# Retention in chunks of 128 instead of 256 tokens, with seven f32 accumulators, and the sample projections moved up

## The chip, the cores and the metric

The kernel runs as one program on all 8 cores of one Trainium2 chip. Each core works on its own share of the data and no core waits for another. The time is the device time in microseconds (us) of the slowest core. The engines are named as in the profile: PE (TensorE, matmuls; PEld are its weight loads), DVE (VectorE), ACT (ScalarE), POOL (GpSimd) and SP (SyncE, which here only issues DMAs).

## The reference, cut to what matters

One layer of a hybrid decoder serves 8 prompts of 2048 tokens and 128 short sequences ("samples") of 8 tokens. Every layer has three branches (retention, a short convolution, cross-attention into memory), which are merged by gates and projected. The change is in the retention branch alone:

```python
def step(S, blk):                       # chunks of RET_CHUNK = 128 tokens
    qc, kc, vc = blk
    s = jnp.einsum('bihd,bjhd->bhij', qc, kc) * inner[None]
    o = (jnp.einsum('bhij,bjhe->bihe', s, vc)
         + jnp.einsum('bihd,bhde->bihe', qc, S) * q_dec[None, :, :, None])
    S = (S * chunk_dec[None, :, None, None]
         + jnp.einsum('bjhd,bjhe->bhde', kc * k_dec[None, :, :, None], vc))
    return S, o
...
o = o * lax.rsqrt(jnp.mean(o * o, axis=-1, keepdims=True) + EPS) * ret_norm_g
```

q and k are rotated (rotary embedding) before this; there are 4 heads with 256 key and 256 value channels. S is the recurrent state of a head, 256 x 256 numbers. The result does not depend on the length of a chunk, since the formula is exact for any length, so a kernel is free to choose it. The samples go through the same formula with one chunk of 8 tokens and a state from memory, which is also written back.

## The kernel before

Each core takes one prompt (2048 tokens, in 4 groups g of 512) and 16 samples (128 tokens in all). The stages run one after the other: normalisation and transposes, the convolution branch with its projection, the memory branch with its projection (`projM`), the retention branch, its projection (`projR`), and the output projection. A small planner (`Plan`) records every operation in program order. Each engine executes its own operations strictly in that order; the planner adds a semaphore wait where an operation reads or overwrites what another engine has written or still reads. A tile is tracked as a whole or in blocks, so a wait can be wider than the data needs.

PSUM, which takes the results of PE, has 8 banks. Six of them (`psf`) are f32 accumulators of 128 x 512, two (`psh`) take transposes. `falloc` and `ffree` hand out the accumulators first in, first out, while the program is built. So it is fixed beforehand which earlier user each accumulator had, and PE waits until the last reader of that user is done.

The retention stage is a loop over i = 0 to 15, that is 4 heads h times 4 groups g. I call one turn of it a period, and number its steps:

1. `prot(i, 256)`: the K projection (16 matmuls of 512 columns into two accumulators). DVE then multiplies by cosine and sine (L1107, four operations of 128 x 512) and POOL subtracts and adds (L1110, L1113). This is the K rotation.
2. `fins`: for the period before, DVE multiplies the normalised output by the gate (L1335, four operations) and so frees its two accumulators.
3. `qdec`: POOL multiplies q by its decay (L1245, two operations of 128 x 512). The table comes by DMA (`tables`, L1088 and L1089).
4. Four `vg_tile` (8 matmuls of 512 columns each): values and gates. ACT copies the values (L1255) and takes the SiLU of the gates (L1256) into `gsg1`, which `fins` reads; so ACT's first SiLU of a period waits for `fins`. After the third tile come the 8 transposes of K (`k_trans`), which ACT scales into `kdt1` (L1266, four operations).
5. `r_scores`: k times q for two chunks of 256 tokens, as three blocks of 128 x 128 each, and the mask on DVE (L1282).
6. `tail(i - 1)`: 8 transposes of the output of the period before, which ACT scales into `ob` (L1238).
7. `kv_state`, twice: the new contribution to the state on PE; DVE updates the f32 state `S32` (L1296, or the copy L1299 for the first chunk of a head). `kv_cast` is ACT's bf16 copy of `S32` (L1304). It reads what the next update overwrites, so update, cast and next update go one after the other. The second cast of a period is recorded only after step 10.
8. `prot(i + 1, 0)`: the Q projection of the next period and its rotation, as in step 1.
9. The samples' step: ACT casts their state (`s_cast`, L1164, two operations of 128 x 1024), PE multiplies (`s_out`, L1175) and computes the update (`s_upd`, two calls with two accumulators each), DVE adds it (L1191), SP writes it out and loads the next (`s_load`).
10. `o_chunk`, twice: 14 matmuls of 256 columns into two accumulators; ACT takes squares (L1200), DVE and POOL make the scale (L1202, L1204).

In the first period of a head (g = 0) the samples' q, k and v projections (`samp_a`) stand between the second and third `vg_tile`, and `samp_b` (transposes of their k, the masked copy `kdm` on DVE (L1148), scores and mask (L1157)) and `samp_d` (the samples' output, L1225) stand after step 7. `samp_a(0)` runs ahead of the loop. At the end of a head SP writes `S32` to memory (`nrp`, L1307), and the first state of the next head (L1299) must wait for that write. `mm` (L416) and `tr` (L419) are the helpers under which every matmul and transpose stands in the profile.

## Time and profile before

| | us |
|---|---|
| median of 3 runs | 1253.17 (1251.75 to 1255.77) |
| the profiled execution, its own time | 1262.68 |
| its span on the slowest core (core 1) | 1261.1 |
| spans of all cores | 1238.0 to 1261.1 |
| retention loop on core 1, first K projection to the end of step 10 of i = 15 | 718.36 to 1074.81 of the span |

The profile is one execution. Its times run from the first instruction of core 1. In a timeline a row gives the start, the length, the engine, the line, the operation with its output and inputs, how many instructions are merged, and in brackets how long the engine stood idle before it and which operation ended that. Engine busy times on core 1 are PE 1190.1, DVE 585.2, ACT 461.1 and POOL 332.6 us.

### The profile page before, as it was taken

To read this page: it belongs to the slowest core of one execution; us is meant where nothing else is said; L and a number is where in the kernel's file an instruction comes from. 1 tells how busy PE (TensorE), PEld (TensorE's weight loads), DVE (VectorE), ACT (ScalarE), POOL (GpSimd) and SP (SyncE) were. 2 spreads that over 40 slices of the span, in tenths; PEclk is the share of its full clock that TensorE was granted. 3 is DMA by queue.
4 is the path that set the end of the run, shared out by engine and by line. 5 is a ranking of instruction groups with operands and counts; after the bars stand their busy time and mean duration, and the time that the engine had idled before them with its cause. 6 is when DMAs were issued, how large, how long until landed. Compare 5 with 4: busy or idle time off the path is not lost.

```text
span 1261.1 us, 22033 instructions; the slowest of 8 cores (1238.0 to 1261.1 us)
## 1 busy us (share of the span) xinstructions
PE 1190.1 (94%) x7140; PEld 605.1 (48%) x7140; DVE 585.2 (46%) x1058; ACT 461.1 (37%) x1010; POOL 332.6 (26%) x424
## 2 busy tenths in 40 slices
PE   3889999999999999999999999989989799999997
PEld 1444444445554554554444544545545445444443
DVE  3764444442222355556212356556565565322266
ACT  3442233322222444444211254545445346322233
POOL 2332222221000111011333434435334344333300
PEclk9999999999999999999999999989999999999989
DMA  9734111112555686974421033724734633811074
GB/s 219 189 85 67 35 34 35 34 34 39 100 101 101 121 135 114 150 120 82 114 52 34 15 104 128 197 96 137 201 118 145 159 126 106 246 35 34 2 253 164
DMA packets 38000, 134.34 MB, mean 107 GB/s; under 512 B 4736, under 2 KB 8960, under 8 KB 33024
## 3 DMA queue, kind: packets, MB, share of 16 engines
q0 software_dynamic: 10080, 56.63, 27.0%
q1 hardware_dynamic: 27808, 76.30, 18.4%
q8 instruction: 60, 0.98, 0.3%
q14 instruction: 52, 0.43, 0.1%
HBM read 160.56 MB, written 28.98 MB: 150 GB/s over the span
## 4 chain that ended last, share of the span: by engine, by line
PE 75%; DVE 7%; DMA 6%; ACT 5%; issue 4%; SPq 1%; POOL 1%; DVEq 0%; ACTq 0%; POOLq 0%
PE psf L416 73%; DVE tf L1107 3%; DMA pms<-c_maskX 2%; DMA nrp<-arF 2%; DMA arF<-c_cos 1%; PE psh L419 1%; DMA mgd<-xp 1%; ACT th L944 1%; ACT ob L1238 1%; ACT arH L1304 1%; ACT mgd L476 1%; DVE th L953 1%; DVE mgd L485 0%; DVE ssb L940 0%; ACT arH L1164 0%
## 5 line engine op out<-in xcount | busy, mean ns | idle before, releaser
L416 PE MATMUL psf<-hT,w 128*128 128x512 bf16 (+1 forms) x3456 | 694.1, 355 | 3.1 <-ACT hT L499 1.5
L416 PEld LDWEIGHTS psf<-hT,w 128*128 128x128 bf16 x3456 | 315.7, 99 | 336.4 <-issue 44.9
L416 PE MATMUL psf<-ob,w 128*128 128x512 bf16 (+1 forms) x960 | 200.1, 352 | 0.0
L556 ACT ACTIVATE tf<-psf,hbg 128x512 f32<-128x512 f32 (+1 forms) x95 | 60.2, 633 | 210.7 <-PE psf L416 206.7
L416 PEld LDWEIGHTS psf<-ob,w 128*128 128x128 bf16 x960 | 87.8, 99 | 93.5 <-issue 12.0
L416 PE MATMUL psf<-w,hT 128*128 128x512 bf16 (+1 forms) x608 | 130.3, 368 | 1.1 <-ACT th L944 1.1
L567 DVE SCALAR_TENSOR_TENSOR tf<-tf,psf 128x512 f32<-128x512 f32 (+1 forms) x79 | 48.0, 607 | 176.2 <-PE psf L416 168.0
L571 POOL TENSOR_TENSOR mgd<-tf,mgd 128x512 bf16<-128x512 f32 (+1 forms) x79 | 78.8, 1005 | 160.1 <-DVE tf L567 160.1
L1107 DVE TENSOR_TENSOR tf<-psf,arF 128x512 f32<-128x512 f32 (+1 forms) x160 | 95.7, 610 | 29.0 <-POOL arH L1110 7.4
L416 PEld LDWEIGHTS psf<-w,hT 128*128 128x128 bf16 x608 | 59.3, 99 | 59.9 <-issue 6.1
L1110 POOL TENSOR_TENSOR th<-tf 128x512 bf16<-128x512 f32 x32 | 40.7, 1270 | 157.2 <-DVE tf L1107 122.2
L397 POOL DMA_DIRECT2D w<-wb x38 | 21.9, 577 | 171.2 <-PE psf L416 170.9
L416 PE MATMUL psf<-w,mgd 128*128 128x512 bf16 x272 | 62.2, 394 | 0.0
L416 PE MATMUL psf<-arH 128*128 128x256 bf16 (+1 forms) x232 | 39.8, 284 | 17.6 <-DVE tf L1107 15.0
L1282 DVE TENSOR_TENSOR arH<-psf,pms 128x256 bf16<-128x256 f32 x64 | 22.9, 358 | 64.3 <-PE psf L416 59.3
L1255 ACT CAST arH<-psf 128x256 bf16<-128x256 f32 x64 | 23.6, 369 | 67.5 <-PE psf L416 66.8
L416 PEld LDWEIGHTS psf<-w,mgd 128*128 128x128 bf16 x272 | 27.4, 101 | 34.4 <-issue 10.9
L1113 POOL TENSOR_TENSOR th<-tf 128x512 bf16<-128x512 f32 x32 | 40.7, 1271 | 4.9 <-DVE arH L1335 0.4
L944 ACT ACTIVATE th<-psf,ssb 128x256 bf16<-128x256 f32 x64 | 30.4, 474 | 27.0 <-DVE ssb L940 16.4
L1245 POOL TENSOR_TENSOR th<-th,pms 128x512 bf16<-128x512 bf16 x32 | 37.2, 1161 | 5.9 <-DMA pms<-c_qdecX 3.6
L419 PE MATMUL psh<-idb,mgd 128*128 128x128 bf16 x136 | 12.4, 245 | 26.5 <-DVE mgd L485 26.5
L1256 ACT ACTIVATE xbuf<-psf 128x256 f32<-128x256 f32 x64 | 24.6, 385 | 31.7 <-DVE arH L1335 26.9
(180 smaller groups left out, 1183.5 us busy)
## 6 DMA issues: line engine op xcount, KB each, us to landing
w<-wb POOLq DMA_DIRECT2D x38, 1024.0 KB, 10.8
mgd<-xp SPq DMA_DIRECT2D x16, 512.0 KB, 11.9
arH<-cmk POOLq DMA_DIRECT2D x12, 512.0 KB, 17.1
arH<-cmv POOLq DMA_DIRECT2D x10, 512.0 KB, 11.8
gaux<-sret SPq DMA_DIRECT2D x8, 512.0 KB, 4.4
xbuf<-sret SPq DMA_DIRECT2D x8, 512.0 KB, 5.1
stgt<-sret SPq DMA_DIRECT2D x8, 512.0 KB, 4.6
hbt<-sret SPq DMA_DIRECT2D x8, 512.0 KB, 5.7
```

Source lines behind the costliest of these rows:

```text
L416: P.op('pe', lambda e: e.matmul(out, lhsT=lhsT, rhs=rhs, start=start, stop=stop), reads=reads, writes=[wbuf])
L419: P.op('pe', lambda e: e.transpose(out=out, in_=in_, identity=ident), reads=reads + [B_id], writes=[wbuf])
L556: P.op('act', lambda e, fg=fg, ti=ti, n=n, bcol=bcol: e.activation(out=tf[ti][:, 0:n], in_=psf[fg][:, 0:n], func=AF.Tanh, bias=hbg[:, bcol ...
L567: P.op('dve', lambda e, fy=fy, ti=ti, t2=t2, n=n: e.scalar_tensor_tensor(out=tf[t2][:, 0:n], in0=tf[ti][:, 0:n], scalar=1.0, in1=psf[fy][: ...
L571: P.op('pool', lambda e, t2=t2, n=n, fc=fc, g=g: e.tensor_tensor(out=mgd[:, fc, sl(g)], in0=tf[t2][:, 0:n], in1=mgd[:, fc, sl(g)], op=ALU. ...
L944: P.op('act', lambda e, c=c, f=fs[hf]: e.activation(out=th_[pi][:, c * 256:(c + 1) * 256], in_=psf[f][:, (c % 2) * 256:(c % 2) * 256 + 256 ...
L1107: P.op('dve', lambda e, t=t, p_=p_, c_=c_: e.tensor_tensor(out=tf[t][:, 0:n], in0=p_, in1=c_, op=ALU.mult), reads=[B_psf[fps[f]], Bcs], wr ...
L1110: P.op('pool', lambda e: e.tensor_tensor(out=lo, in0=tf[b1][:, 0:n], in1=tf[b2][:, 0:n], op=ALU.subtract), reads=[B_tf[b1], B_tf[b2]], wri ...
L1113: P.op('pool', lambda e: e.tensor_tensor(out=hi_, in0=tf[a1][:, 0:n], in1=tf[a2][:, 0:n], op=ALU.add), reads=[B_tf[a1], B_tf[a2]], writes= ...
L1245: P.op('pool', lambda e, dch=dch: e.tensor_tensor(out=th_[qdi][:, dch * 512:(dch + 1) * 512].rearrange("p (c i) -> p c i", c=2), in0=th_[q ...
L1255: P.op('act', lambda e: e.copy(out=vtm1[:, c, :], in_=psf[f][:, 0:256]), reads=[B_psf[f]], writes=B_vtm1)
L1256: P.op('act', lambda e: e.activation(out=gsg1[:, c, :], in_=psf[f][:, 256:512], func=AF.Silu), reads=[B_psf[f]], writes=B_gsg1)
```

## The change

A chunk is now 128 tokens (`RC2 = 128`), so a period has four chunks with four state updates in place of two. The scores are four blocks of 128 x 128 in one accumulator with one masking operation, and `qdec` and the scaling of `kdt1` are one operation each. The state has four bf16 copies. One of the two transpose banks becomes a seventh f32 accumulator. The samples' projections stand right behind K (q and k in one accumulator, rotated in four operations of 256 columns), `samp_b` stands behind the second `vg_tile`, the two `s_cast` stand behind the first and the second `vg_tile`, and `tail` stands behind the Q projection. The write of `nrp` is issued right behind the last state update of a head.

```diff
-RC2 = 256
+RC2 = 128
...
+        psf.append(psh[1][:].bitcast(F32)); B_psf.append(B_psh[1])
+        free_h[:] = [0]
+        free_f.append(6)
...
         def samp_a(h):
-            proj_rot(h, 0, slice(LP, NT), 128, csS, BL_csS, qS[:, 0:128], qS[:, 128:256], BL_qS)
-            proj_rot(h, 256, slice(LP, NT), 128, csS, BL_csS, kS[:, 0:128], kS[:, 128:256], BL_kS)
+            fq = falloc()
+            for z in range(4):
+                off = (z // 2) * 256 + (z % 2) * 128
+                for k in range(8):
+                    mm(psf[fq][:, z * 128:z * 128 + 128], WA[:, k, off:off + 128], hT[:, k, LP:NT], k == 0, k == 7, [B_hT, BWA], B_psf[fq])
...
+            for (t, d, z) in ((0, 0, 0), (1, 1, 1), (2, 0, 1), (3, 1, 0)):
+                P.op('dve', lambda e, t=t, d=d, z=z: e.tensor_tensor(out=tv[t], in0=pv_[:, :, d, :], in1=cb[z], op=ALU.mult),
+                     reads=[B_psf[fq], BL_csS], writes=[B_tf[ts[t]]])
...
             fv = falloc()
-            for (o_, w0) in ((0, 0), (256, 256)):
-                for k in range(8):
-                    mm(psf[fv][:, o_:o_ + 256], hT[:, k, LP:NT], WB[:, k, w0:w0 + 256], k == 0, k == 7, [B_hT, BWB], B_psf[fv])
+            for k in range(8):
+                mm(psf[fv][:], hT[:, k, LP:NT], WB[:, k, :], k == 0, k == 7, [B_hT, BWB], B_psf[fv])
...
 # r_scores
+            fs = falloc()
             for c in range(4):
+                for dch in range(2):
+                    o_ = dch * 512 + c * 128
+                    mm(psf[fs][:, c * 128:(c + 1) * 128], th_[ki][:, o_:o_ + 128], th_[qi][:, o_:o_ + 128], dch == 0, dch == 1,
+                       [B_th[ki], B_th[qi]], B_psf[fs])
+            P.op('dve', lambda e: e.tensor_tensor(
+                out=stm1.rearrange("p (c t) -> p c t", c=4), in0=psf[fs][:, 0:512].rearrange("p (c t) -> p c t", c=4),
+                in1=maskX.unsqueeze(1).to_broadcast([128, 4, RC2]), op=ALU.mult),
+                reads=[B_psf[fs], B_mq], writes=B_stm1)
...
 # the loop
+            if g == 0 and h > 0:
+                samp_a(h)
             qdec(qi, qdi)
             vg_tile(WB, BWB, g, 0)
+            s_cast(h, g, 0)
             vg_tile(WB, BWB, g, 1)
-            if g == 0 and h > 0:
-                samp_a(h)
+            s_cast(h, g, 1)
+            if g == 0:
+                samp_q(h)
+                samp_b(h)
...
-            r_scores(ki, qi, sx)
-            if i > 0:
-                tail(i - 1)
+            r_scores(ki, qi)
...
-            kv_state(h, 2 * g)
-            kv_cast(h, 2 * g)
-            kv_state(h, 2 * g + 1)
-            if g == 0:
-                if h > 0:
-                    samp_d(h - 1)
-                samp_b(h)
+            for c in range(4):
+                kv_state(h, 4 * g + c)
+                if c < 3 or g == 3:
+                    kv_cast(h, 4 * g + c)
+            if g == 0 and h > 0:
+                samp_d(h - 1)
...
             if i < 15:
                 qn = prot(i + 1, 0)
...
-            s_cast(h, g)
+            if i > 0:
+                tail(i - 1)
             s_out(h, g)
...
-            fo = [o_chunk(2 * g, qdi, sx), o_chunk(2 * g + 1, qdi, sx)]
-            kv_cast(h, 2 * g + 1)
+            fo = [o_pair(h, g, qdi, 0), o_pair(h, g, qdi, 1)]
+            if g < 3:
+                kv_cast(h, 4 * g + 3)
```

`o_pair` makes two chunks of output in one accumulator: for each chunk one matmul of masked scores times values and two of decayed q times the state copy `Sbf[c]`.

## Rows read from the trace of the kernel before

**Rows 1.** Span and granted TensorE clock of the slowest core

```profile
core 1: 1261.1 us, clock 0.972
```

**Rows 2.** Windows: the loop, then periods 4, 8, 12 and 6

```profile
core 1: us, PE busy (x) PEld busy (x) DVE busy (x) ACT busy (x) POOL busy (x), PEclk, DMA share, GB/s
718.36:1074.81 356.45, 325.29 (x2165) 176.47 (x2163) 214.66 (x405) 173.79 (x426) 145.30 (x136) 0.96 0.48 137
801.25:830.42 29.17, 25.35 (x179) 14.58 (x177) 17.80 (x39) 13.15 (x34) 11.03 (x13) 0.89 0.51 140
892.37:921.19 28.82, 25.52 (x179) 14.75 (x177) 17.90 (x39) 13.00 (x34) 11.05 (x13) 0.91 0.53 147
981.94:1014.13 32.19, 24.62 (x180) 14.09 (x178) 17.74 (x39) 13.01 (x34) 10.97 (x13) 0.90 0.49 133
852.09:872.07 19.98, 18.79 (x128) 10.13 (x126) 12.70 (x24) 10.73 (x27) 8.39 (x8) 1.00 0.38 132
```

**Rows 3.** Timeline of PE, period 6 and the start of period 7

```profile
864.30 1.03 PE L416 MATMUL psf<-arH 128*128 128x256 bf16 x8
865.17 3.62 PE L416 MATMUL psf<-hT,w 128*128 128x512 bf16 x16
...
870.53 0.27 PE L416 MATMUL psf<-arH 128*128 128x256 bf16 x1 [1.06 <-DVE tf L1107]
...
872.07 3.62 PE L416 MATMUL psf<-hT,w 128*128 128x512 bf16 x16
```

**Rows 4.** Timeline of DVE, period 6 into 7

```profile
863.50 1.75 DVE L1282 TENSOR_TENSOR arH<-psf,pms 128x256 bf16<-128x256 f32 x4 [3.83 <-PE psf L416]
865.16 0.68 DVE L1296 SCALAR_TENSOR_TENSOR arF<-arF,psf 128x512 f32<-128x512 f32 x1
866.66 0.69 DVE L1296 SCALAR_TENSOR_TENSOR arF<-arF,psf 128x512 f32<-128x512 f32 x1 [0.82 <-ACT arH L1304]
867.31 0.69 DVE L1107 TENSOR_TENSOR tf<-psf,arF 128x512 f32<-128x512 f32 x1
868.17 2.21 DVE L1107 TENSOR_TENSOR tf<-psf,arF 128x512 f32<-128x512 f32 x3 [0.17 <-DVE tf L1107]
870.30 1.47 DVE L1191 SCALAR_TENSOR_TENSOR gaux<-gaux,psf 128x512 f32<-128x512 f32 x2
...
877.55 2.25 DVE L1335 SCALAR_TENSOR_TENSOR arH<-psf,ssb,xbuf 128x256 bf16<-128x256 f32 x4
```

**Rows 5.** Timeline of ACT, periods 6 and 7

```profile
867.40 1.04 ACT L1164 CAST arH<-xbuf 128x1024 bf16<-128x1024 f32 x1
...
879.89 0.38 ACT L1256 ACTIVATE xbuf<-psf 128x256 f32<-128x256 f32 x1 [2.02 <-DVE arH L1335]
880.17 0.37 ACT L1255 CAST arH<-psf 128x256 bf16<-128x256 f32 x1
...
883.68 0.47 ACT L1266 ACTIVATE arH<-psh,arF 128x256 bf16<-128x256 bf16 x1 [0.37 <-ACT arH L1266]
884.05 0.36 ACT L1255 CAST arH<-psf 128x256 bf16<-128x256 f32 x1
```

**Rows 6.** Waits of period 8 (first of a head): DVE, then PE

```profile
902.90 0.29 DVE L1107 TENSOR_TENSOR tf<-psf,arF 128x128 f32<-128x128 f32 x1 [1.13 <-POOL arH L1110]
912.59 0.69 DVE L1299 COPY arF<-psf 128x512 f32<-128x512 f32 x1 [1.98 <-DMA nrp<-arF]
...
916.26 0.27 PE L416 MATMUL psf<-arF 128*128 128x256 bf16 x1 [1.16 <-DVE arF L1157]
```

**Rows 7.** Timeline of SP's queue, end of period 3 into 4

```profile
806.10 0.33 SPq L1089 DMA_DIRECT2D pms<-c_qdecX  x1
...
815.49 0.42 SPq L1307 DMA_DIRECT2D nrp<-arF  x1
```

**Rows 8.** Windows of half clock after period 4, of the last wait of period 6

```profile
827.00:833.80 6.80, 5.96 (x21) 2.62 (x22) 3.82 (x7) 1.93 (x8) 3.57 (x3) 0.50 0.48 167
...
868.72:872.07 3.35, 2.29 (x31) 1.65 (x31) 3.11 (x6) 0.51 (x1) 2.13 (x2) 1.00 0.00 0
```

More of the change, by code:

```diff
@@ L196, in _consts @@
     qdecX = np.exp(lg64[:, None] * (r[None, :] + 1.0))
-    kdecX = np.zeros((128, 8))
-    for h in range(4):
-        for c in range(2):
-            kdecX[:, h * 2 + c] = np.exp(lg64[h] * (RC2 - 1.0 - (c * 128 + j))) / 16.0
+    kdecX = np.exp(lg64[None, :] * (RC2 - 1.0 - j[:, None])) / 16.0
     cdX = np.exp(lg64 * RC2)
@@ L1136, in samp_a, with samp_q @@
             ffree(fv)
+        def samp_q(h):
+            P.tag = 'ret_s'
             qd = qdecS[:, h, :]
@@ L1159, in samp_b, with s_cast @@
             ffree(fs)
-        def s_cast(h, s_):
-            for pp in range(2):
-                n = (h * 4 + s_) * 2 + pp
-                P.op('act', lambda e, pp=pp, n=n: e.copy(out=Sqf[:, pp * 1024:(pp + 1) * 1024], in_=pr[n % 4]),
-                     reads=B_pr[n % 4], writes=BL_Sqb[pp * 4:(pp + 1) * 4])
+        def s_cast(h, s_, pp):
+            n = (h * 4 + s_) * 2 + pp
+            P.op('act', lambda e: e.copy(out=Sqf[:, pp * 1024:(pp + 1) * 1024], in_=pr[n % 4]),
+                 reads=B_pr[n % 4], writes=BL_Sqb[pp * 4:(pp + 1) * 4])
         def s_out(h, s_):
@@ L1243, in qdec @@
         def qdec(qi, qdi):
-            for dch in range(2):
-                P.op('pool', lambda e, dch=dch: e.tensor_tensor(
-                    out=th_[qdi][:, dch * 512:(dch + 1) * 512].rearrange("p (c i) -> p c i", c=2),
-                    in0=th_[qi][:, dch * 512:(dch + 1) * 512].rearrange("p (c i) -> p c i", c=2),
-                    in1=qdecX.unsqueeze(1).to_broadcast([128, 2, RC2]), op=ALU.mult),
-                    reads=[B_th[qi], B_mq], writes=[B_th[qdi]])
+            P.op('pool', lambda e: e.tensor_tensor(
+                out=th_[qdi][:].rearrange("p (n i) -> p n i", n=8), in0=th_[qi][:].rearrange("p (n i) -> p n i", n=8),
+                in1=qdecX.unsqueeze(1).to_broadcast([128, 8, RC2]), op=ALU.mult),
+                reads=[B_th[qi], B_mq], writes=[B_th[qdi]])
         def vg_tile(WB, BWB, g, c):
@@ new lines, in k_trans, with r_scores @@
+            P.op('act', lambda e: e.activation(
+                out=kdt1.rearrange("p c e -> p (c e)"), in_=psh[hi][:], func=AF.Copy, scale=kdecX[:, h:h + 1]),
+                reads=[B_psh[hi]] + BL_kdecX, writes=BL_kdt)
+            hfree(hi)
+        def r_scores(ki, qi):
+            fs = falloc()
+            for c in range(4):
+                for dch in range(2):
+                    o_ = dch * 512 + c * 128
[5 more added lines that the diff above has]
+                reads=[B_psf[fs], B_mq], writes=B_stm1)
+            ffree(fs)
@@ L1287, in kv_state @@
         def kv_state(h, n):
-            cc = n % 2
+            c = n % 4
             fkv = falloc()
             for dch in range(2):
-                for jb in range(2):
-                    c = cc * 2 + jb
-                    mm(psf[fkv][:, dch * 256:dch * 256 + 256], kdt1[:, c, dch * 128:(dch + 1) * 128], vtm1[:, c, :],
-                       jb == 0, jb == 1, [BL_kdt, B_vtm1], B_psf[fkv])
+                mm(psf[fkv][:, dch * 256:dch * 256 + 256], kdt1[:, c, dch * 128:(dch + 1) * 128], vtm1[:, c, :],
+                   True, True, [BL_kdt, B_vtm1], B_psf[fkv])
@@ L1300, in kv_state @@
             ffree(fkv)
         def kv_cast(h, n):
-            if n < 7:
-                P.op('act', lambda e: e.copy(out=Sbf[(n + 1) % 2].rearrange("p c e -> p (c e)"), in_=S32),
-                     reads=[BL_S32], writes=[B_Sbf[(n + 1) % 2]])
+            if n < 15:
+                P.op('act', lambda e: e.copy(out=Sbf[(n + 1) % 4].rearrange("p c e -> p (c e)"), in_=S32),
+                     reads=[BL_S32], writes=[B_Sbf[(n + 1) % 4]])
             else:
@@ L1357, in build_nc @@
             fins = []
+            if g == 0 and h > 0:
+                samp_a(h)
+            P.tag = 'ret'
             qdi = tha()
```

65 lines of the change are left out of this document (27 added, 38 removed).

## The prediction

> **What bounds the kernel now.** I read the spans of the cores first, then windows by stage, then the waits, then one period engine by engine. The slowest core is core 1 [rows 1]. The loop is 356.45 us long, and PE is busy in 325.29 of them, so 31 us are idle [rows 2]. Outside it PE is busy 865 of 905 us (1190.1 of the page less 325.3, 1261.1 less 356.45), and the change touches nothing there except the last `tail`. No other engine is near full: DVE 215, ACT 174. The loop is bound by PE plus the waits in which PE's next accumulator or operand comes late. That is why the order of work on DVE and ACT, and not their load, decides.
>
> A period in the middle of a head takes 19.98 us, with 18.79 us of PE [rows 2]. Its one large wait stands before `o_chunk`: 1.06 us, ended by the rotation of Q on DVE [rows 3]. The reason is the order of the accumulators: `o_chunk`'s first one is that of the second half of Q, so all four rotation operations must be over. They start after the second state update [rows 4]. The first period of a head costs much more: 29.17, 28.82 and 32.19 us (periods 4, 8 and 12) [rows 2]. There the first state copy waits for the write of `nrp`, the rotations of the samples wait for POOL, and PE waits for the samples' mask [rows 6].
>
> **A middle period after the change.** I write times from the start of its K projection. The accumulators' order follows from counting `falloc` and `ffree`: after the change `s_upd` takes those of the four `kv_state`, in order, and `o_pair` takes exactly the two of the Q projection.
>
> PE's own work: scores 8 x 128 columns in place of 4 x 256 and 4 x 128, output 12 matmuls of 256 in place of 14. Eight matmuls of 256 take 0.87 us (864.30 to 865.17), 0.109 each [rows 3]. So the scores save 512 columns, 0.22, and the output 0.22 us. That is 0.43 us a period, if PE is the bound. It isn't, as follows.
>
> (a) To the state updates. `fins` ended 7.73 us after K (879.80 from 872.07) and ACT's first SiLU followed at 7.82 [rows 3 to 5]. I keep 7.6, since the squares of the first pair now lie further ahead. ACT must then get through, in order: SiLU, `s_cast` (its two copies follow each other by 0.95, 866.45 to 867.40, of 1.04 each [rows 5]), two more tiles at 0.77 each, the second `s_cast`, the scaling of K and the last values' copy. The scaling was four operations of 0.47, 0.56 apart, so 2.26. As one of 1024 columns it is not in the trace. It is bounded by 1.04 (the cast of the same size [rows 5]) from below and 2.26 from above; I take 1.1, since its size is that of the cast. Sum: 7.6 + 0.3 + 0.95 + 0.77 + 0.95 + 0.77 + 1.1 + 0.35 = 12.8, so `kv_state` starts at 12.85. PE is there at 11.55, when its own last value tile allows it (10.8 plus the copy); 1.3 us of wait. Before, it started at 12.2 to 12.5 (864.30 [rows 3]). The casts that were hidden behind the Q projection now stand in front of the state.
>
> (b) The state chain. Update, cast, update takes 1.50 us per link (865.16 to 866.66), and DVE, a strict queue, stands idle 0.82 of it for ACT [rows 4]. A state update works on the whole state, so it is no shorter for half the tokens. First update at 12.85 + 0.5 = 13.35, the fourth three links later at 17.85, its end at 18.54. Before, there was one link. What is queued behind it on DVE is the rotation of Q; what waits for that is `o_pair`.
>
> (c) Rotation and output. The rotation takes 3.07 (867.31 to 870.38) [rows 4], so it ends at 21.6. Meanwhile PE has done Q (13.7 to 17.15), `tail` (0.44), `s_out` and half of `s_upd`; its fourth accumulator is that of the fourth `kv_state`, so it waits until 18.7. The first pair waits for the second rotation operation, until 20.25; the second pair for the fourth, until 21.75, and takes 6 x 0.109 = 0.65. The next K starts at 22.4 to 22.45. Its accumulators come from the first `s_upd` operation on DVE, 0.7 after the rotation: no further wait. **A middle period is 22.45.**
>
> Eleven periods are of this kind (i = 1, 2, 3, 5, 6, 7, 9, 10, 11, 13, 14). They took 223.4 us, the loop's 356.45 less the three first periods (90.2) [rows 2] and less periods 0 and 15 (22.5 and 20.4, from one start of K to the next). They will take 247.0: **+23.6**.
>
> **First periods of a head (4, 8, 12).** They took 90.2 us [rows 2]. The samples' projections cost PE 1.75 (32 x 128 columns) and 1.7 us as now, so they end at 6.9. They no longer stand behind `qdec` on POOL, the wait of 1.13 [rows 6] goes; but their rotation stands behind K's and `fins` on DVE and ends at 10.2, POOL at 11.0, so `samp_b` costs PE 0.7. The masked copy (128 x 1024, I take 1.2 us, near two updates of 512 at 0.68) holds the only transpose bank until 13.3, so `k_trans` waits 0.4. `kv_state` starts at 16.4. SP reaches `nrp` right after the `qdecX` table (806.10) instead of 815.49 [rows 7], 9 us earlier, so the wait of 1.98 for it [rows 6] and the longer one in period 12 end, and so does the 1.16 for the samples' mask. From 16.4 the chain is as in (b) and (c): last update ends 22.1, rotation 25.2, next K at 26.0. `samp_d` now stands behind three casts on ACT and holds the transpose bank until 22.0; `tail` waits 1.3 us for it, still under cover of the rotation. Three times 26.0 is 78.0: **-12.2**.
>
> **The ends.** Period 0 (22.5 by K) has no `fins` and no casts in its way late: 21.4, **-1.1**. Period 15 has no rotation of Q: 20.2 for 20.4, **-0.2**. After it, `tail(15)` must wait for the one transpose bank, two ACT operations: **+1.1**. `qdec` as one POOL operation stays hidden, its result is needed 10 us later. `s_cast` earlier needs its load 12 us earlier; that load was issued two periods ahead, so nothing. The tables are smaller DMAs in the same queue: nothing.
>
> Sum: +23.6 - 12.2 - 1.1 - 0.2 + 1.1 = +11.2.
>
> **The clock.** After period 4 PE ran at 1.2 GHz (granted 0.50) for 6.8 us, [rows 8], after a period with 3.8 us of idle PE (29.17 less 25.35) [rows 2] that lie mostly in its last 5 us. A middle period before the change keeps 2.4 GHz through its wait [rows 8]. After it, the waits at `s_upd` and before both pairs come to 2.7 us within 3.6. That is close to the pattern which dropped the clock behind the samples. A drop of 3.4 us costs 1.7. I allow one such drop in about ten periods, +2. The ends of the range are none (0) and one in every middle period (+19).
>
> So +13 on the 1253.2 median is **1266**. Against the profile's own numbers: 1262.7 becomes 1276 and the span 1261 becomes 1274; the profiled run is 9.5 above the median, and I carry the difference, not the level.
>
> **Rivals.**
>
> *The half-speed rival* (slower still). Every middle period loses the clock once: 1253 + 11 + 19 = 1283. For it: the gaps lie as close as those behind period 4. Against: PE runs Q at full density right before. The Trainium skill (TensorE: Matmul & The Clock Gate, "A second HAM failure mode: psum-queue depth-cycling") describes a kernel whose short idles between groups, from cycling through PSUM banks, made the clock swing in this way. In this trace it swung only behind the samples.
>
> *The ACT rival* (no change). If ACT's casts do not delay `kv_state` (it starts at 11.55), a period is 1.3 shorter, 11 x 1.3 = 14.3, and the whole is -3 to -1: 1250 to 1252. Against: ACT's queue is in order and each length is in the rows.
>
> *The seventh accumulator cures the wait* (faster). The 1.06 us before `o_chunk` recur in all middle periods; with one accumulator more PE could run ahead, and the extra state links would hide behind Q. Then a middle period is at most the old one less 0.43, 19.55: 11 x 19.55 = 215, -8.4. With the heads at 22.9 (26.0 less 3.0) -21.5, together -30: 1223. It decides once the extension per middle period stays under 1.0 us (11.2 / 11); I have 2.1 over the old mean. Against: the accumulators that `o_pair` gets are Q's own, so the seventh does not loosen this wait. The Trainium skill (Perfetto Trace Analysis, "Optimization Strategy") says that the same gap repeating can mean too few buffers in PSUM, which speaks for this rival; by the rule the gap should shrink.
>
> **How the numbers follow.** Forecast 0.65, with its own range 1258 to 1274 (2 us on each first period, 0.4 on each middle one). Half-speed rival 0.13, ACT rival 0.12, seventh accumulator 0.10. Likeliest 1266. Leaving out 2 in 10 (the seventh-accumulator rival, and the outer parts of the others), the range is 1250 to 1282. About 0.3%, 3.8 us, is what a measurement of this kernel can tell from no change. Faster by more than that: 0.10 + 0.04 from the ACT rival = 0.14. Within: 0.08 + 0.04 from the low end of the forecast = 0.12. Slower: 0.74.
>
> **What the profile will show.** Right if: K to K 22 to 23 us in the middle; four L1296 updates (new line) 1.5 apart with ACT's cast as releaser; the rotation of Q starting some 18.5 after K; PE's waits before both pairs ended by that rotation; a wait before `kv_state` ended by ACT; no wait of the first state copy for `nrp`; first periods near 26. Wrong if the updates follow each other by 0.7, if the pairs start without a wait, or if the first periods keep 29.

## The result, and the profile after

The changed kernel takes 1287.49 us (1281.18 to 1416.15, 4 runs) where the kernel before takes 1252.78 (1251.75 to 1255.77) on the same chip: 1.0231 times as long, interval 1.0202 to 1.0261, slower. Two of the four runs (1292.26 and 1416.15) had a lower clock on one die and are not in the ratio; the others took 1281.18 and 1282.71. I had said 1266, with 1282 as the upper end. The direction was right, the size was not.

The profiled execution took 1281.18 us. First the spans and the mean granted clock of the changed kernel's slowest core (7) and of the core in whose trace one period without a loss of clock is read below (1), beside [rows 1].

```profile
core 1: 1266.7 us, clock 0.987
core 7: 1279.5 us, clock 0.977
```

The retention loop ran from 709.1 to 1093.2 on core 7: 384.1 us, against 356.45 [rows 2], so 27.7 more. Over the eight cores it was 375.5 to 384.2, before 351.2 to 357.8; nearly the whole loss lies in the loop. Windows after, with the columns of [rows 2]: on core 7 the loop; on core 1 period 6 and period 8, both at full clock.

```profile
709.10:1093.20 384.10, 331.81 (x2118) 170.68 (x2116) 229.25 (x378) 181.94 (x408) 141.01 (x114) 0.95 0.44 126
```

```profile
848.14:870.23 22.09, 18.88 (x126) 9.85 (x124) 13.27 (x23) 11.24 (x27) 8.21 (x6) 1.00 0.36 119
892.32:919.28 26.96, 22.95 (x171) 12.29 (x169) 19.07 (x33) 13.13 (x31) 10.16 (x9) 1.00 0.40 123
```

PE is busy as long in a middle period as before (18.88, was 18.79 [rows 2]), but the period is 2.11 us longer. The 0.43 us that I had taken off PE's work do not show here; with the waits removed PE is busy 18.45 (last of the combinations below). Where it stands still is in the timeline of PE, core 1, period 6, which answers to [rows 3]. In this kernel's rows `psh` is also the name of the seventh accumulator, and `arF` holds the state and the tables:

```profile
860.89 1.03 PE L413 MATMUL psf<-arH 128*128 128x256 bf16 x8 [1.32 <-ACT arH L1273]
...
866.71 0.37 PE L413 MATMUL psf<-arF 32*128 32x256 bf16 x3 [0.23 <-DVE arF L1308]
868.17 0.27 PE L413 MATMUL psh<-arH 128*128 128x256 bf16 x1 [1.09 <-DVE tf L1109]
...
869.57 0.27 PE L413 MATMUL psf<-arH 128*128 128x256 bf16 x1 [0.56 <-DVE tf L1109]
...
870.23 1.03 PE L413 MATMUL psf<-hT,w 128*128 128x512 bf16 x4
```

There were 1.06 us of waiting here, now there are 3.20 in four places: before `kv_state` for ACT's copy of the last values, in `s_upd` for the last state update, and before each pair for the rotation of Q. The timelines of DVE and ACT of the same period, which answer to [rows 4, 5], name the reason:

```profile
861.38 0.69 DVE L1308 SCALAR_TENSOR_TENSOR arF<-arF,psf 128x512 f32<-128x512 f32 x1 [1.02 <-PE psf L413]
862.88 0.69 DVE L1308 SCALAR_TENSOR_TENSOR arF<-arF,psf 128x512 f32<-128x512 f32 x1 [0.82 <-ACT arH L1316]
864.38 0.69 DVE L1308 SCALAR_TENSOR_TENSOR arF<-arF,psf 128x512 f32<-128x512 f32 x1 [0.81 <-ACT arH L1316]
865.88 0.69 DVE L1308 SCALAR_TENSOR_TENSOR arF<-arF,psf 128x512 f32<-128x512 f32 x1 [0.81 <-PE psh L416]
866.48 0.68 DVE L1109 TENSOR_TENSOR tf<-psh,arF 128x512 f32<-128x512 f32 x1
```

```profile
855.90 1.04 ACT L1184 CAST arH<-gaux 128x1024 bf16<-128x1024 f32 x1
...
857.58 1.04 ACT L1184 CAST arH<-xbuf 128x1024 bf16<-128x1024 f32 x1
...
859.27 1.11 ACT L1283 ACTIVATE arH<-psh,arF 128x1024 bf16<-128x1024 bf16 x1
860.26 0.37 ACT L1273 CAST arH<-psh 128x256 bf16<-128x256 f32 x1
...
865.15 0.62 ACT L1316 CAST arH<-arF 128x512 bf16<-128x512 f32 x1 [0.88 <-DVE arF L1308]
```

The four updates start 1.50 us apart, DVE idle 0.81 to 0.82 before each but the first. The row of the last update names PE as its releaser, which is the profile's choice among several semaphores: PE had written that accumulator by 861.9, and the row starts 0.11 us after ACT's third copy of the state ended (865.77), as the two rows above it do after theirs. The rotation of Q starts 18.3 us after K (866.48 less 848.14). On ACT both casts of the samples' state stand in front of the scaling of K.

Two things I had sized wrongly. The first is the clock, which I had counted at 2 us. Windows of core 7 after: period 6, the 3.4 us before the clock fell at its end, and the 3.4 us at the lower clock.

```profile
853.10:876.76 23.66, 20.44 (x126) 10.33 (x124) 13.25 (x23) 11.24 (x25) 8.09 (x7) 0.93 0.33 112
872.70:876.10 3.40, 1.53 (x12) 0.95 (x13) 3.12 (x6) 1.83 (x6) 1.06 (x1) 1.00 0.00 0
876.10:879.50 3.40, 3.40 (x12) 1.51 (x11) 2.17 (x5) 1.38 (x6) 2.36 (x3) 0.50 0.43 172
```

PE was busy 1.53 of 3.4 us through the waits before the pairs, then ran 3.4 us at 1.2 GHz (granted 0.50), into the next K projection. Period 6 also begins inside such a stretch, of period 5, and takes 23.66 and not 22.09. Core 7 has eleven such stretches in the loop, 37.5 us in all; over all cores it was 17.1 to 37.5, before 13.7 to 27.3. Before, they began only in the periods with the samples' transposes (0, 4, 8, 12). Now none begins in 4, 8 or 12, and nearly all begin 20 to 24 us after a K projection, at or behind the waits of the pairs, on core 7 in ten of the eleven middle periods. Half of the time at 0.50 that lies in the middle periods is 6.3 to 12.9 us on the eight cores, and these periods together are 6.8 to 12.7 us longer than eleven clean ones. In the trace before, core 1 ran another 20.7 us of its loop at a granted clock of 0.81, most of them in periods 4 and 8; the cores 4 to 7 did not, and their loops are as long.

The second is DVE in the first period of a head. DVE, then POOL, then PE, core 1, period 8 after:

```profile
903.12 2.54 DVE L1161 TENSOR_TENSOR qms<-arH,qdecS 128x128 bf16<-128x128 bf16 x2 [1.04 <-POOL arH L1147]
905.58 1.22 DVE L1169 TENSOR_TENSOR arF<-psh,arF 128x1024 bf16<-128x1024 bf16 x1
908.58 0.29 DVE L1178 TENSOR_TENSOR arF<-psf,arF 128x128 bf16<-128x128 f32 x1 [1.78 <-DMA arF<-c_maskSf]
```

```profile
902.97 2.15 POOL L1264 TENSOR_TENSOR th<-th,pms 128x1024 bf16<-128x1024 bf16 x1
```

```profile
906.94 0.61 PE L416 MATMUL psh<-idb,th 128*128 128x128 bf16 x8 [1.33 <-DVE arF L1169]
```

L1161 is `samp_q`, the samples' decay on DVE, two operations of 128 x 128. They took 2.54 us together; the masked copy L1169, which holds the transpose bank, is late by 1.85 us (they take 0.69 together where POOL is idle, as an experiment below shows), and `k_trans` waits 1.33. DVE then waits for the DMA of the samples' mask (1.78 here, 0 to 3.4 over the cores), which I had not priced; in this kernel no wait of PE comes of it. The write of `nrp` went as I had said: SP issues it 0.4 us behind the `qdecX` table, and no state copy waits for it.

### The profile page after: what moved, and what is told of

Its sections match the earlier page's. It is cut to its first block, busy times and chain, and to the rows that moved or that the text cites. A ratio compares the mean times of both kernels' runs of the same rounds, so it can differ in the third digit from the quotient of the medians.

```text
span 1279.5 us, 21808 instructions; the slowest of 8 cores (1262.7 to 1279.5 us)
## 1 busy us (share of the span) xinstructions
PE 1184.9 (93%) x7084; PEld 595.1 (47%) x7084; DVE 598.9 (47%) x1026; ACT 469.1 (37%) x994; POOL 328.0 (26%) x400
## 4 chain that ended last, share of the span: by engine, by line
PE 78%; DVE 9%; issue 5%; ACT 5%; POOL 2%; DMA 1%; SPq 0%; DVEq 0%; ACTq 0%; POOLq 0%
PE psf L413 71%; PE psh L413 5%; DVE tf L1109 3%; PE psh L416 2%; DMA mgd<-xp 1%; DVE arF L1308 1%; ACT arH L1316 1%; ACT th L941 1%; ACT arH L1283 1%; ACT mgd L473 1%; DVE qms L1161 1%; DVE th L950 1%; DVE tf L1141 0%; ACT arH L1273 0%; DVE ssb L937 0%
## 5 line engine op out<-in xcount | busy, mean ns | idle before, releaser
L413 PE MATMUL psf<-hT,w 128*128 128x512 bf16 (+1 forms) x3328 | 665.7, 354 | 5.3 <-ACT hT L496 3.7
L413 PEld LDWEIGHTS psf<-hT,w 128*128 128x128 bf16 x3328 | 303.4, 99 | 326.2 <-issue 31.8
L413 PE MATMUL psf<-ob,w 128*128 128x512 bf16 (+1 forms) x904 | 185.0, 348 | 0.0
L413 PE MATMUL psf<-w,hT 128*128 128x512 bf16 (+1 forms) x480 | 107.1, 372 | 1.1 <-ACT th L941 1.1
L1109 DVE TENSOR_TENSOR tf<-psf,arF 128x512 f32<-128x512 f32 x108 | 73.5, 690 | 24.4 <-PE psf L413 12.9
L413 PEld LDWEIGHTS psf<-w,hT 128*128 128x128 bf16 x480 | 45.7, 98 | 50.1 <-issue 2.0
L1316 ACT CAST arH<-arF 128x512 bf16<-128x512 f32 x60 | 37.0, 617 | 58.5 <-DVE arF L1308 42.7
L1308 DVE SCALAR_TENSOR_TENSOR arF<-arF,psf 128x512 f32<-128x512 f32 x50 | 34.4, 688 | 42.7 <-ACT arH L1316 27.2
L413 PE MATMUL psf<-w,mgd 128*128 128x512 bf16 x232 | 52.9, 388 | 0.0
L413 PEld LDWEIGHTS psf<-arH 128*128 128x128 bf16 x168 | 15.4, 99 | 45.6 <-issue 43.6
L416 PE MATMUL psh<-idb,mgd 128*128 128x128 bf16 x136 | 12.4, 245 | 25.6 <-DVE mgd L482 25.6
```

The source lines that it names most:

```text
L413: P.op('pe', lambda e: e.matmul(out, lhsT=lhsT, rhs=rhs, start=start, stop=stop), reads=reads, writes=[wbuf])
L416: P.op('pe', lambda e: e.transpose(out=out, in_=in_, identity=ident), reads=reads + [B_id], writes=[wbuf])
L1109: P.op('dve', lambda e, t=t, p_=p_, c_=c_: e.tensor_tensor(out=tf[t][:, 0:n], in0=p_, in1=c_, op=ALU.mult), reads=[B_psf[fps[f]], Bcs], wr ...
L1308: P.op('dve', lambda e: e.scalar_tensor_tensor(out=S32, in0=S32, scalar=CDX[h], in1=psf[fkv][:, 0:512], op0=ALU.mult, op1=ALU.add), reads= ...
L1316: P.op('act', lambda e: e.copy(out=Sbf[(n + 1) % 4].rearrange("p c e -> p (c e)"), in_=S32), reads=[BL_S32], writes=[B_Sbf[(n + 1) % 4]])
```

## The experiments

Each was timed beside the kernel before on the same chip, in three rounds, the one called "made to wait" in five. "Middle" is a middle period at full clock, "first" the first periods of heads 1 to 3, "half" the time at granted clock 0.50 in the loop; each over the eight cores of one profiled execution. Differences of whole times below are worked out from the ratios, at 1248 us for the kernel before.

| kernel | ratio to before (interval) | middle | first | half |
|---|---|---|---|---|
| before | 1 | 19.98 | 27.2 to 32.2 | 13.7 to 27.3 |
| after | 1.0231 (1.0202 to 1.0261) | 22.09 | 27.0 to 28.7 | 17.1 to 37.5 |
| casts back | 1.0147 (1.0123 to 1.0172) | 21.02 | 27.2 to 31.0 | 20.5 to 27.3 |
| casts at K | 1.0097 (1.0080 to 1.0115) | 21.03 | 27.2 to 30.7 | 17.1 to 23.9 |
| two state buffers | 0.9957 (0.9944 to 0.9971) | 20.11 | 26.2 to 31.4 | 0 to 17.1 |
| filler | 1.0191 (1.0160 to 1.0221) | 22.07 | 28.6 to 31.6 | 0 to 17.1 |
| samples' part alone | 1.0005 (0.9994 to 1.0016) | 19.98 | 27.9 to 33.8 | 10.2 to 20.5 |
| the same, mask early | 0.9946 (0.9925 to 0.9968) | 19.98 | 26.7 to 30.7 | 10.2 to 17.1 |
| after, mask early | 1.0219 (1.0183 to 1.0255) | 22.09 | 26.9 to 28.4 | 27.3 to 34.1 |
| two state buffers, mask early | 0.9838 (0.9819 to 0.9857) | 20.11 | 25.0 | 0 |
| and casts at K | 0.9750 (0.9731 to 0.9770) | 19.06 | 23.6 to 25.3 | 0 |
| and decay of q recorded later | 0.9749 (0.9726 to 0.9772) | 19.06 | 23.6 to 25.2 | 0 |
| and made to wait | 0.9709 (0.9693 to 0.9724) | 19.05 | 23.6 (one of 24: 25.6) | 0 to 3.4 |
| 256 tokens with the rest | 0.9818 (0.9781 to 0.9855) | 19.98 | 24.3 to 25.1 | 0 to 3.4 |

**Casts back.** Only the place of `s_cast` is undone.

```diff
             vg_tile(WB, BWB, g, 0)
-            s_cast(h, g, 0)
             vg_tile(WB, BWB, g, 1)
-            s_cast(h, g, 1)
...
+            s_cast(h, g, 0)
+            s_cast(h, g, 1)
             P.tag = 'ret'
             if i > 0:
                 tail(i - 1)
```

> The changed kernel with the two casts of the samples' state back behind the Q projection. Theory (ACT's queue holds back the state updates by 1.3 us, a strict chain of four updates and casts follows, and the clustered waits drop the clock): kv_state starts about 11.6 us after K instead of 12.75, a clean middle period falls from 22.09 to about 20.9, the half-clock time stays or falls a little; total 12 to 18 us below the changed kernel, 1264 to 1270. Rival (the casts' place does not matter, the chain of updates alone sets the period): within 3 us of the changed kernel, since the casts then queue behind the chain and delay the samples' matmuls.

The wait before `kv_state` fell from 1.32 to 0.27 and the clean middle period from 22.09 to 21.02, 1.05 and 1.07 us. The casts now end late at their own reader, as the waits of PE on core 3 of this kernel show (total, times, longest):

```profile
PE psf L1195 <- ACT arH L1184: 30.8, 16, 2.6
```

`s_out` waits 1.99 us in a middle period, in the place of the waits before the pairs; the rotation of Q comes late anyhow. The clock still falls (20.5 to 27.3 us at half). The whole is 10 us below after, less than the 12 to 18 expected: the first periods grew to 27.2 to 31.0. In 17 of the 24, PE now waits up to 3.2 us for the samples' masking (L1178), which waits for the mask's DMA.

**Two state buffers.** The state is read from one f32 buffer and written to the other in turn, so an update need not wait for ACT's cast of the one before. The second buffer lies in `ob`, where head 3 comes last.

```diff
+        S2 = [ob[:, 7, 1024:2048].bitcast(F32), S32]; BS2 = [B_ob[7][2:4], BL_S32]
...
-                P.op('dve', lambda e: e.scalar_tensor_tensor(out=S32, in0=S32, scalar=CDX[h], in1=psf[fkv][:, 0:512], op0=ALU.mult, op1=ALU.add),
+                P.op('dve', lambda e: e.scalar_tensor_tensor(out=S2[n % 2], in0=S2[(n + 1) % 2], scalar=CDX[h], in1=psf[fkv][:, 0:512], op0=ALU.mult, op1=ALU.add),
...
```

> The changed kernel with two f32 state buffers used in turn, so that an update need not wait for the cast of the one before. It computes the same. Theory (the chain of 1.50 us a link in front of the rotation of Q is the main loss): four updates follow each other by about 0.7, the rotation of Q starts when its matmuls are done, about 15.8 us after K instead of 18.4; a middle period falls to about 19.7, the waits before the output pairs nearly vanish, and with them the half clock in middle periods; total 35 to 42 us below the changed kernel, 1240 to 1247, under the kernel before. Rival (accumulators or the single transpose bank are the limit): the gap before the pairs stays near 1 us and the gain is under 10 us.

DVE in a middle period of this kernel, core 1:

```profile
852.79 0.69 DVE L1309 SCALAR_TENSOR_TENSOR ob<-arF,psf 128x512 f32<-128x512 f32 x1 [1.02 <-PE psf L413]
853.59 0.69 DVE L1309 SCALAR_TENSOR_TENSOR arF<-ob,psf 128x512 f32<-128x512 f32 x1
854.46 0.69 DVE L1309 SCALAR_TENSOR_TENSOR ob<-arF,psf 128x512 f32<-128x512 f32 x1 [0.17 <-DVE arF L1309]
855.32 0.69 DVE L1309 SCALAR_TENSOR_TENSOR arF<-ob,psf 128x512 f32<-128x512 f32 x1 [0.17 <-DVE ob L1309]
```

The updates follow each other by 0.80 to 0.87 in place of 1.50. From the first start to the fourth it is 2.53 us and was 4.50, 1.97 less; the period lost 1.98, to 20.11 and not to the 19.7 expected. Before the pairs 0.35 us of waiting is left in a clean period (0.70 at most), and no middle period lost the clock on any core, although the 1.32 before `kv_state` is still there. So it is the idle time late in the period that costs the clock. This one edit turns the slower kernel into one that is 0.4% faster than before, 34 us below after (35 to 42 expected). Its first periods (26.2 to 31.4) wait for the samples' mask: PE 0.6 to 5.2 us in all 24.

**Filler.** After, plus 16 transposes of the identity in each period where PE waits. They compute nothing that is read. They write the transpose bank, so the first eight wait for `tail`'s copy out of it, 0.44 us in a clean period.

```diff
-            fo = [o_pair(h, g, qdi, 0), o_pair(h, g, qdi, 1)]
+            fill(8)
+            fo = [o_pair(h, g, qdi, 0)]
+            fill(8)
+            fo.append(o_pair(h, g, qdi, 1))
```

> The changed kernel with 16 transposes of the identity more in each period, 8 before each output pair, which write the free transpose bank and are read by nobody. They only keep TensorE busy while it waits. Theory (clustered waits drop the clock to 1.2 GHz for 3.4 us, 1.6 us each, in most middle periods): the half-clock time in the loop falls from 17 to 37 us to under 12, middle periods all near 22.1 to 22.3, total 8 to 14 us below the changed kernel, about 1270, although PE does more. Rival (the drops come from the wait before the state update, or cost nothing because PE waits anyway): total same or up to 5 us above.

Spans and windows of core 4 of this kernel: the core, and the same period as above.

```profile
core 4: 1265.3 us, clock 0.998
```

```profile
846.60:868.70 22.10, 19.95 (x142) 10.90 (x141) 13.30 (x23) 11.26 (x27) 8.20 (x6) 1.00 0.35 119
```

PE does 1.07 us more in the period (19.95 for 18.88) and the period is as long as a clean one of after. The eleven middle periods took 243.5 to 244.9 us, in after 249.8 to 255.7. So the idle time before the pairs is what costs the clock, and it costs after's middle periods 7 to 13 us (249.8 to 255.7 less 11 times 22.09). The whole is only 0.4% below after, 5 us and not 8 to 14, with intervals that overlap: by the ratio alone the rival that the drops cost nothing is not excluded, and the windows of the middle periods decide. The rest is lost in the first periods (28.6 to 31.6), also on cores that never lose the clock. Core 4, first period of head 1, DVE and PE:

```profile
813.83 0.29 DVE L1178 TENSOR_TENSOR arF<-psf,arF 128x128 bf16<-128x128 f32 x1 [4.58 <-DMA arF<-c_maskSf]
```

```profile
814.26 0.38 PE L413 MATMUL psf<-arH 128*128 128x256 bf16 x2 [1.11 <-DVE arF L1178]
```

It is the samples' mask again, hidden in after; the fillers there wait another 0.93 us for the transpose bank. A filler with the mask loaded early was not tried.

**Samples' part alone.** The kernel before, with 256 tokens, and only the new `samp_a`, `samp_q`, `samp_b` in their new places.

```diff
+            if g == 0 and h > 0:
+                samp_a(h)
+            P.tag = 'ret'
             qdi = tha()
...
             vg_tile(WB, BWB, g, 1)
-            if g == 0 and h > 0:
-                samp_a(h)
+            if g == 0:
+                samp_q(h)
+                samp_b(h)
...
-                samp_b(h)
```

> The kernel before with one part of the change alone: the samples' projections behind K with q and k in one accumulator, and the samples' transposes and mask behind the second value tile. Chunks of 256, six accumulators, two transpose banks, casts and tail where they were. Theory: middle periods stay at 19.98, the first periods of heads 1 to 3 fall from 27 to 32 us to 24.5 to 26.5 (the wait for the write of the last head's state stays, so period 12 falls least); total 6 to 13 us below the kernel before, 1240 to 1247. Rival (the move only brings the masked copy and its transposes to a worse place): same as before within 3 us.

It gained nothing, because a new wait took the place of the old ones. DVE on core 7 of this kernel:

```profile
812.02 0.29 DVE L1177 TENSOR_TENSOR arF<-psf,arF 128x128 bf16<-128x128 f32 x1 [11.30 <-DMA arF<-c_maskSf]
```

The samples' mask is issued from SP's queue behind the tables and the outputs that wait for their data, and now it is needed a few us after its issue. A DMA belongs to a step that is moved, and here it was left where the queue is full.

**The same, mask early.** The mask is loaded in the second period of the head before.

```diff
+            if g == 1 and h < 3:
+                mask_load(h + 1)
             ki = prot(i, 256)
```

> The kernel before with the samples' part of the change, and the samples' mask loaded in the second period of the head before, not at the end of SP's queue. Theory (moving the samples brought nothing because DVE then stood up to 11 us at the samples' mask, whose DMA was issued last): the first periods of heads 1 to 3 fall from 29 to 33 us to 25 to 27, the wait for the mask's DMA is gone; total 9 to 15 us below the kernel before, 1232 to 1238. Rival (the write of the old state is then waited for just as long): same as the kernel before, within 4 us.

The mask's wait is gone and the kernel 0.5% faster than before, 7 us and not 9 to 15 (first periods 26.7 to 30.7, not 25 to 27). The waits of DVE and of PE, core 5 of this kernel:

```profile
DVE arF L1321 <- DMA nrp<-arF: 11.7, 3, 5.2
```

```profile
PE psf L1197 <- ACT arH L1186: 14.5, 6, 5.7
```

The first state copy of a head waits for the write of `nrp`; behind it on ACT wait the copy for the matmuls and the casts of the samples' state, and for these `s_out`. The wait that the mask's had covered is next in line. The kernel with 256 tokens at the end of this section issues that write early and casts behind K: its first periods are 24.3 to 25.1.

**After, mask early.** The same edit on the changed kernel.

> The changed kernel, with one edit: the samples' mask is loaded in the second period of the head before. If the late mask was what kept the first periods of a head at 28 us and not at the 26.0 that I predicted: first periods 26 to 27, all else as after, 1274 to 1278 (ratio 1.017 to 1.022 of the kernel before). Rival (the first periods are long because of the slow samples' operations and the half clock): 27.5 to 28.5, 1279 to 1283 (ratio 1.021 to 1.026).

The first periods stayed at 27.6 to 28.4 where the clock is lost and 26.95 where it is not, as in after. The ratio fits both expectations, the first periods only the rival's: the 1.78 us for which DVE waits for the mask are hidden there, and the 1.33 behind the slow `samp_q` are not.

**Casts at K.** The two `s_cast` stand right behind the K projection, ahead of ACT's first copy of values.

```diff
             ki = prot(i, 256)
+            s_cast(h, g, 0)
+            s_cast(h, g, 1)
...
             vg_tile(WB, BWB, g, 0)
-            s_cast(h, g, 0)
             vg_tile(WB, BWB, g, 1)
-            s_cast(h, g, 1)
```

> The changed kernel with the two casts of the samples' state recorded right behind the K projection, where ACT stood idle for about 4 us. Theory (the casts between the value tiles hold back kv_state by 1.3 us and nothing else waits for them): kv_state starts about 11.6 us after K, a clean middle period is 20.8 to 21.0, no wait of the samples' matmuls for a cast; total 14 to 20 us below the changed kernel, 1256 to 1264 against 1247 for the kernel before. Rival (ACT's queue is not what kv_state waits for, so the wait stays 1.3): same as the changed kernel.

The middle period is 21.03, as with the casts put back, and `s_out` does not wait: in after, ACT stood idle 4.08 us there, before its first copy of values. Period 15 fell to 19.49, and the whole is 17 us below after, as expected (14 to 20). The waits before the pairs are the same as in after (1.09 and 0.56) and the clock still falls (17.1 to 23.9 us at half).

**The combinations.** Two state buffers with the early mask, and then the casts at K on top.

> The changed kernel with two state buffers used in turn, and the samples' mask loaded early. Theory: against the run with two state buffers alone the first periods fall from 26 to 31 us to about 24 to 25, middle periods stay at 20.1; total 8 to 14 us below that run, 1229 to 1235. Rival (the first periods are held by the one transpose bank): less than 4 us.

> The changed kernel with two state buffers, the early mask and the casts right behind K. Theory (with the chain, the casts and the mask out of the way a middle period is PE's own work plus about 0.3 us): middle periods 18.5 to 19.0, first periods 23 to 24; total 1210 to 1220, at least 25 us below the kernel before. Rival (one of the other waits, the rotation of Q or the single transpose bank, takes the place of those removed): middle periods stay above 19.6, total 1225 or more.

The middle period is 20.11 with the first and 19.06 with both. The two savings add up: 22.09 less 1.98 less 1.05 is 19.06. With the first the first periods are 25.03 on all cores, without any half clock, where they were 26.2 to 31.4 with the late mask: 15 us less for the whole, a little more than expected.

**Is `samp_q` slow because of POOL?** In the last version the first periods came in two lengths on different cores, 25.03 and 23.6. I recorded the decay of q (`qdec`) behind the samples' part there.

```diff
             qdi = tha()
-            qdec(qi, qdi)
+            if g > 0:
+                qdec(qi, qdi)
...
                 samp_q(h)
                 samp_b(h)
+                qdec(qi, qdi)
```

> The version with everything in it (two state buffers, early mask, casts at K: 0.975 of the kernel before), but in the first period of a head the decay of q on POOL stands behind the samples' part. Theory (the samples' decay on DVE is slow, 1.27 us for each of two operations, because POOL runs its long bf16 operation at the same time): each takes 0.4 to 0.5 us, first periods shrink from 25.0 to 23.5 to 24.5 us, time 1212 to 1216 (ratio 0.971 to 0.974). Rival (the operation is slow for another reason, its shape or its neighbours on DVE): it stays near 1.27 us, first periods stay at 25.0 or grow, since the output now waits for the decayed q: 1216 to 1220.

No difference: POOL has nothing else to do and still starts at the same moment, since no wait holds it. The edit did not do what it was for. But the two lengths can be told apart in its trace. DVE, then POOL, on core 1 of this kernel, in the first periods of head 1 (25.03) and of head 2 (23.56):

```profile
791.94 2.53 DVE L1164 TENSOR_TENSOR qms<-arH,qdecS 128x128 bf16<-128x128 bf16 x2 [1.03 <-POOL arH L1150]
...
874.15 0.69 DVE L1164 TENSOR_TENSOR qms<-arH,qdecS 128x128 bf16<-128x128 bf16 x2 [1.03 <-POOL arH L1150]
```

```profile
791.79 2.13 POOL L1267 TENSOR_TENSOR th<-th,pms 128x1024 bf16<-128x1024 bf16 x1
...
875.22 2.13 POOL L1267 TENSOR_TENSOR th<-th,pms 128x1024 bf16<-128x1024 bf16 x1 [1.17 <-DMA pms<-c_qdecX]
```

Where POOL's long operation is held up by the late table, `samp_q` is short. So I made POOL wait for it: `B_mx` is the tile that `samp_q` writes, and `qdec` now counts it among what it reads.

```diff
-                qdec(qi, qdi)
+                qdec(qi, qdi, [B_mx])
```

> As the version before it (decay of q on POOL behind the samples' part in the first period of a head), but POOL's long operation now also waits until the samples' decay on DVE is done; before, it still started 0.15 us ahead of it. Theory (the DVE operation with both inputs in SBUF stands still until a running POOL operation that reads SBUF is over, and is short by itself): each of the two takes 0.29 us in every first period of a head on every core, the first periods are all 23.5 to 23.7 us in place of 25.0, the loop is 4.4 us shorter than with 25.0, time 1211 to 1214 (ratio 0.969 to 0.973). Rival (its length has another cause, and the overlap in the rows is a coincidence): it still takes 2.1 us in most periods, first periods 25.0, time 1215 to 1218 (ratio 0.973 to 0.977).

DVE, then POOL, of this kernel, core 1, first period of head 1:

```profile
793.83 0.69 DVE L1164 TENSOR_TENSOR qms<-arH,qdecS 128x128 bf16<-128x128 bf16 x2 [1.03 <-POOL arH L1150]
794.43 1.22 DVE L1172 TENSOR_TENSOR arF<-psh,arF 128x1024 bf16<-128x1024 bf16 x1
```

```profile
794.66 2.13 POOL L1267 TENSOR_TENSOR th<-th,pms 128x1024 bf16<-128x1024 bf16 x1 [0.94 <-DVE qms L1164]
```

Each of the two operations took 0.29 us, on all cores, in all three heads. 23 of the 24 first periods are 23.55 to 23.65; the one of 25.60 lies on the core with 3.4 us of half clock. This is the fastest kernel of the study, 0.9709 of before.

**256 tokens with the rest.** The kernel before with the samples' new part, the early mask, the casts behind K and the early write of `nrp`, but with its chunks and its six accumulators.

> The kernel before, with its chunks of 256 tokens, and with everything that helped and has nothing to do with the chunk: the samples' new part, their mask early, the samples' casts right behind K, the write of the last state issued early. It shows what the chunk of 128 and the seventh accumulator are worth with the waits removed. If the chunk as such gains only PE's 0.4 us a period and the wait for the rotation of Q is the same: middle periods 19.4 to 19.98, first periods 25 to 27, time 1222 to 1234 (ratio 0.978 to 0.987), above the 0.975 of the same with 128. If the chunk is worth nothing: the same 0.975.

It takes 0.9818 of before, with first periods of 24.3 to 25.1, a little shorter than expected. Its middle periods are 19.98 as ever, with the 1.06 us before the output; those with 128 tokens are 19.06. So the chunk of 128 with the seventh accumulator is worth 0.92 us a period once its two losses are taken away: PE is busy 18.45 in place of 18.77, and idle 0.61 in place of 1.21 (waits of 0.34 before the output and 0.27 before `kv_state`, against 1.06 before the output). The 0.9750 of the same with 128 is clear of 0.9818. The kernel with 128 also has the second state buffer and its `tail` behind the Q projection; what the chunk, the seventh accumulator and the place of `tail` are worth each was not tried.

## Why the prediction was wrong in size

**Steps (a), (b), (c) of a middle period hold.** `kv_state` 12.75 us after K (I said 12.85), first update 13.24 (13.35), 1.50 per link (1.50), the scaling of K 1.11 (1.1), rotation begun at 18.3 and over at 21.3 (21.6), pairs at 20.03 and 21.43 (20.25 and 21.75), the period 22.09 (22.45). The 0.36 are an earlier start of the rotation and its 2.94 in place of 3.07. Two experiments price the two steps by themselves: 1.05 us for the casts in front of the state, 1.98 us for the longer chain.

**The step that failed is the clock.** I wrote "I allow one such drop in about ten periods, +2"; there were eleven drops in the sixteen periods of the slowest core, ten of them begun in its eleven middle periods. On this core the eleven middle periods took 255.7 us where eleven clean ones take 243.0, so 12.7; another 3.5 lie in the first periods (84.4 less three times 26.96), 1.45 in period 15 (22.09, clean 20.64) and 0.6 in period 0. Together 18.2 us, where half of its 37.5 us at granted 0.50 is 18.8. I had the trace's one hint before me, a drop behind idle time of 3.8 us spread over five [rows 2, 8], had put the new waits at 2.7 in 3.6, and had called it close to that pattern; I should then have taken the half-speed rival as likely as my own. Its mechanism is the one that the runs show. That its 1283 also meets the time (1281.18 and 1282.71) is in part luck, since its other terms were off in both directions, as the sum below shows. My range ended at 1282, one short of it. The Trainium skill (TensorE: Matmul & The Clock Gate, "A second HAM failure mode: psum-queue depth-cycling") describes a kernel whose clock swings through short idles between its groups of matmuls. There they come from cycling through PSUM banks, here from an operand that is late; the filler and the second state buffer agree as to the idles: less idle time in the same place, no drop begun in a middle period.

**The second term mis-sized is the first period of a head.** I took 26.0; a clean one is 26.96. I had `k_trans` waiting 0.4 us, it waits 1.33. The difference of 0.93 is `samp_q`: I let it take what the kernel before shows, two of 0.43 to 0.50, and did not look at what POOL would be doing at its new place. Even those two were waits for POOL: they begin beside its operations of 0.45 us and end 0.15 after them. The rest of that step held, the early `nrp` and the samples' projections out of POOL's way but for 0.36. That the mask's DMA cost PE nothing was luck, though. I had given no term to it, and in the kernels whose periods are shorter it cost PE up to 5.2 us in a first period.

**The sum again.** Middle periods -4.0 by the steps and +12.7 by the clock; first periods +2.9 and +3.5; period 0 +0.5; period 15 +1.9 (21.4 and 20.2 forecast). That is +17.5 above the +10.1 which I had for the loop without the clock, so +27.6; measured 27.7. The `tail` behind `samp_d` waits 1.3 us in most first periods and 1.1 after the loop, as I said.

**The other rivals.** The ACT rival (`kv_state` at 11.55) did not occur; without the casts in the way it would have been worth 1.05 us a period, not enough. The seventh accumulator did not cure the wait before the output (1.06, now 1.09 and 0.56), since the pairs wait for the rotation in Q's own accumulators. The Trainium skill (Perfetto Trace Analysis, "Optimization Strategy") says that a gap which repeats can mean too few buffers, in SBUF or in PSUM. Here it was a buffer indeed, yet not in PSUM, where I had looked, but in SBUF: one more for the state took 1.98 us out of every period.

## What to carry to other kernels

Halving a chunk doubles the links of a recurrence, and a link costs its fixed operations, not its tokens: give the state a second buffer before you shorten the chunk, so that the copy for the matmuls stands beside the chain and not in it. Price a new cluster of waits on PE with the clock as well: where it looks like the stretch ahead of a drop that the trace already shows, count that drop in every period. And a step that is moved takes its DMAs and its neighbours on other engines with it: look at what each queue does at the new place.

## What the runs showed of the hardware

**DVE stands still for a POOL operation.** `samp_q` reads both inputs from SBUF. Beside no POOL operation each of its two parts takes 0.29 us. When POOL's 128 x 1024 operation, which reads SBUF too, runs already (2.14 us), the first part ends 0.15 us after POOL does and takes 2.14 or 2.15 us, in every first period of heads 1 to 3 of the changed kernel, on every core. In the version with 256 tokens, where that work is two operations (2.46 us together), each of the two parts mostly takes 1.16 to 1.20. In the kernel before they stood beside operations of 0.45 us and took 0.43 to 0.50. The other order occurs too: on core 2 of the version with `qdec` recorded later both engines started together once, DVE took its 0.29, and POOL 2.30 in place of 2.14. The masked copy (L1172 above, one input from PSUM) takes 1.22 us beside the same POOL operation and 1.22 without it. The Trainium skill (SBUF — State Buffer, "Who interferes with whom") says that a DVE instruction with two inputs in SBUF and a GpSimd instruction that reads SBUF exclude each other for a whole instruction, whichever starts first; these rows agree, the masked copy included.

**The clock falls after a few short waits, with PE otherwise busy.** No wait in those periods is longer than 1.5 us. 1.53 us of work in 3.4 us (window 872.70 to 876.10) came before a stretch at 1.2 GHz; with fillers in the same waits, and with 0.35 to 0.70 us of waiting left there, it stayed at 2.4 GHz in all middle periods. A single wait of 1.32 before `kv_state`, earlier in the period, did not cost the clock in any middle period of the kernel with two state buffers. Not all cores lost it equally often with the same program and the same waits (17.1 to 37.5 us), and the runs don't show why.
